# First expert's rows from one-hot products instead of a gather, in a two-layer decoder trunk with sorted experts

## What is computed

```python
for layer in range(2):
    u = rms_norm(h, norm_mix[layer]) * (1 + sc1) + sh1
    h = h + g1 * mixer(u)            # layer 0: windowed attention and convolution; layer 1: pooling
    u = rms_norm(h, norm_ffn[layer]) * (1 + sc2) + sh2
    h = h + g2 * grouped_moe(u)      # 16 experts, each token goes to 2 of one group of 4
return rms_norm(h, norm_final)

# grouped_moe, per expert e, for the tokens that chose it
hid = silu(t @ w_gate[e]) * (t @ w_up[e])      # 1024 -> 256
out = out + gates[:, e] * (hid @ w_down[e])    # 256 -> 1024
```

## Time and profile before

| | |
|---|---|
| median of 3 runs | 689.59 us (689.57 to 692.98) |
| profiled execution | 691.79 us, span 690.10 us |
| TensorE busy | 636.4 us (92%) |
| VectorE busy | 358.3 us (52%) |
| ScalarE busy | 171.5 us (25%) |
| GpSimd busy | 96.9 us (14%) |
| mean granted clock of TensorE | 0.965 of full |

### The profile page before, as it was taken

The page is one execution under the profiler, slowest core; times in us unless marked ns, Lnnn a source line. Parts: engine busy times, 40 slices in busy tenths (PEclk is TensorE's granted clock), DMA queues, the critical chain, the costliest instruction groups (busy, mean ns, idle before and its releaser), DMA issues. The chain is left out here.

```text
span 690.1 us, 8415 instructions
## 1 busy us (share of the span) xinstructions
PE 636.4 (92%) x2897; PEld 328.6 (48%) x2897; DVE 358.3 (52%) x714; ACT 171.5 (25%) x437; POOL 96.9 (14%) x84
## 2 busy tenths in 40 slices
PE   4899989999899995889999999999678999999994
PEld 3455434444444442445455554468345455555441
DVE  4117698799996237863432222264776233223325
ACT  5000322323333421211122211242421122122223
POOL 0010001000000004113132312100021212222210
PEclk9999989999999996989999999999989999999997
DMA  9999998878889415799999998374789899999726
GB/s 326 361 367 371 384 318 289 328 263 293 311 307 393 160 64 186 249 410 312 322 345 371 359 321 272 92 274 183 305 304 393 278 309 354 370 367 364 253 41 244
DMA packets 68568, 203.76 MB, mean 295 GB/s; under 512 B 9633, under 2 KB 18965, under 8 KB 68524
## 3 DMA queue, kind: packets, MB, share of 16 engines
q1 hardware_dynamic: 58836, 183.63, 72.3%
q0 software_dynamic: 9040, 18.87, 11.4%
q10 hardware_dynamic: 648, 0.71, 0.3%
HBM read 189.90 MB, written 23.11 MB: 309 GB/s over the span
## 5 line engine op out<-in xcount | busy, mean ns | idle before, releaser
L1877 PE MATMUL ps<-ring,work 128*128 128x512 f32 x288 | 127.8, 595 | 0.0
L949 DVE SCALAR_TENSOR_TENSOR acc<-adaw,cond,acc 128x1024 f32<-128x1024 f32 x70 | 89.8, 1283 | 8.5 <-DMA adaw<-in_w_ada_dram 6.6
L1701 PE MATMUL psY<-xu,ring 128*128 128x512 f32 x192 | 88.0, 612 | 0.0
L1877 PEld LDWEIGHTS ps<-ring,work 128*128 128x128 f32 x288 | 54.3, 191 | 67.1 <-issue 66.8
L1402 DVE TENSOR_TENSOR work<-work,ps 128x256 f32<-128x256 f32 (+1 forms) x32 | 11.9, 372 | 128.6 <-ACT work L854 92.7
L854 ACT ACTIVATE work<-ps 128x256 f32<-128x256 f32 (+1 forms) x32 | 11.0, 344 | 237.7 <-PE ps L1877 175.6
L1915 PE MATMUL psY<-ring,work 128*128 128x512 f32 x144 | 69.8, 630 | 0.0
L1701 PEld LDWEIGHTS psY<-xu,ring 128*128 128x128 f32 x192 | 36.4, 195 | 45.4 <-issue 45.2
L613 POOL DMA_INDIRECT h_dram<-work x20 | 33.2, 1662 | 152.7 <-DVE work L1432 75.4
L847 ACT ACTIVATE work<-psA,modc,scl 128x128 f32<-128x128 f32 (+1 forms) x120 | 42.5, 434 | 48.2 <-PE psA L1854 46.6
L1432 DVE SCALAR_TENSOR_TENSOR work<-psY,work,gbc 128x512 f32<-128x512 f32 x40 | 28.2, 747 | 44.1 <-PE psY L1915 44.1
(11 more groups left out here) (266 smaller groups left out, 782.1 us busy)
## 6 DMA issues: line engine op xcount, KB each, us to landing
adaw<-in_w_ada_dram SPq DMA_DIRECT2D x84, 512.0 KB, 5.3
ring<-in_w_gate_dram SPq DMA_DIRECT2D x48, 512.0 KB
ring<-in_w_up_dram SPq DMA_DIRECT2D x48, 512.0 KB
ring<-in_w_down_dram SPq DMA_DIRECT2D x48, 512.0 KB
xu<-in_w_gate_dram SPq DMA_DIRECT2D x16, 512.0 KB
xu<-in_w_up_dram SPq DMA_DIRECT2D x16, 512.0 KB
xu<-in_w_down_dram SPq DMA_DIRECT2D x16, 512.0 KB
work<-in_w_ada_dram SPq DMA_DIRECT2D x12, 512.0 KB, 9.9
```

The costliest lines, as they stand in the source:

```text
L949: dve.scalar_tensor_tensor(total, adaw[:, n % ABUF, :], cond[:, k:k + 1], total if k else brow[:, :], ALU.mult, ALU.add).then_inc(mac_step, 1)
L1701: ins = pe.matmul(bank, wt, uT[:, k, :], start=(k == 0), stop=(k == KD - 1))
L1877: ins = pe.matmul(gu_ps[j % 2][:, :].rearrange("p (a f) -> p a f", a=2), xgT[:, j % 2, k, :], w_gu(j % 4)[:, :, k, :], start=(k == 0), sto ...
```

## The change

Position 0's rows are no longer gathered and turned. VectorE writes a float32 one-hot of expert 0 (`first_hot`, 128x512, in `brow`), and TensorE multiplies each strided 128x128 piece of `xhat` with it: for each of 8 channel blocks 4 products, one for each tile, summed in PSUM. That gives the turned rows at once. These 32 products stand in `route`, with `token_table(0)` ahead of the fourth block; `first_banked` lets ScalarE start after four blocks. The order of the one-hots and of the tables is now position 1 first, then 0, so that position 1, still gathered, is first in line. `tokens(l, 1)` moves behind VectorE's first half. The last `keep_clock` matmuls go. The memset of `xg` is done in two parts, the first when the mix has read three tiles, the second when it has read the fourth, ahead of GpSimd's wait for `h`. SyncE stores `h` of a tile when `h` is ready and the normed rows of the tile before behind it, and waits for the products before it loads weights over `xhat`. In `first_product` of position 0 the wait for VectorE's half comes at k = 4. The load of the final norm's row counts on `gbc_in` now.

```diff
-HOT = [(0,), (1,), (2, 3), (4, 6), (5,), (7,), (8, 10), (9,), (11,), (12, 13), (14,), (15,)]
-TABLE = [(0,), (1,), (2, 3), (4, 5, 6, 7), (8, 9, 10, 11, 12, 13, 14, 15)]
+HOT = [(1,), (0,), (2, 3), (4, 6), (5,), (7,), (8, 10), (9,), (11,), (12, 13), (14,), (15,)]
+TABLE = [(1,), (0,), (2, 3), (4, 5, 6, 7), (8, 9, 10, 11, 12, 13, 14, 15)]
...
-HOT_BY_TABLE = [1, 2, 3, 6, 12]
+HOT_BY_TABLE = [2, 3, 4, 7, 13]
+HOTS = len(HOT) + 1
...
+        first_hot = brow[:, 0:T * P].rearrange("p (t s) -> p t s", t=T)
...
-                for t in range(T):
-                    sp.wait_ge(xhat_ready, (2 * l + 1) * T + t + 1)
-                    sp.dma_start(h_dram[l][t * P:(t + 1) * P, :], h[:, t, :]).then_inc(h_stored, 16)
-                    sp.dma_start(xhat_dram[l][t * P:(t + 1) * P, :], xhat[:, t, :]).then_inc(xhat_stored, 16)
+                for t in range(T + 1):
+                    if t < T:
+                        sp.wait_ge(h_ready, l * T + t + 1)
+                        sp.dma_start(h_dram[l][t * P:(t + 1) * P, :], h[:, t, :]).then_inc(h_stored, 16)
+                    if t:
+                        sp.wait_ge(xhat_ready, (2 * l + 1) * T + t)
+                        sp.dma_start(xhat_dram[l][(t - 1) * P:t * P, :], xhat[:, t - 1, :]).then_inc(xhat_stored, 16)
...
                 sp.wait_ge(ids_ready, l + 1)
+                sp.wait_ge(xT_banked, l * E + 1)
...
                     load_cols(1)
 
+                    parts = xg.rearrange("p b d -> p (b d)").rearrange("p (c s) -> p c s", s=SEQ)
+                    pool.wait_ge(mix_banked, 2 * (T - 1))
+                    pool.memset(parts[:, :, 0:(T - 1) * P], 0.0).then_inc(xg_clear, 1)
+                    pool.wait_ge(mix_banked, 2 * T)
+                    pool.memset(parts[:, :, (T - 1) * P:SEQ], 0.0).then_inc(xg_clear, 1)
                 pool.wait_ge(h_ready, T * (l + 1))
...
-                    pool.memset(xg[:, :, :], 0.0).then_inc(xg_clear, 1)
-                    pool.wait_ge(xg_clear, 1)
+                    pool.wait_ge(xg_clear, 2)
...
-                for e in range(E):
+                for e in range(1, E):
...
+                dve.tensor_tensor(first_hot, cst[:, C_SLOT:C_SLOT + P].unsqueeze(1).broadcast_to([P, T, P]),
+                                  posm[:, :, 0:1].broadcast_to([P, T, P]), ALU.is_equal).then_inc(onehot_ready, 1)
                 one_hots(l, 0)
                 tokens(l, 0)
                 one_hots(l, 1)
-                tokens(l, 1)
...
                 xT_half(0, 0, 0)
+                tokens(l, 1)
                 room(l)
...
-                token_table(l, 0)
-                keep_clock(1)
+                first_rows_in(l)
+
+            def first_rows_in(l):
+
+                pe.wait_ge(xhat_ready, (2 * l + 2) * T)
+                pe.wait_ge(onehot_ready, l * HOTS + 1)
+                for k in range(KD):
+                    if k == 3:
+                        token_table(l, 0)
+                    for t in range(T):
+                        src = xhat[:, t, :].rearrange("p (a k) -> p k a", k=KD)[:, k, :]
+                        ins = pe.matmul(turned_ps(0)[:, k * P:(k + 1) * P], src, first_hot[:, t, :],
+                                        start=(t == 0), stop=(t == T - 1))
+                    if k == KD // 2 - 1:
+                        ins.then_inc(first_banked, 1)
+                ins.then_inc(xT_banked, 1)
                 token_table(l, 1)
...
-                    pe.wait_ge(xT_dve, l * E + e + 1)
+                    if e:
+                        pe.wait_ge(xT_dve, l * E + e + 1)
...
+                            if e == 0 and k == KD // 2:
+                                pe.wait_ge(xT_dve, l * E + 1)
                             if e == 0 and k == 5:
                                 token_table(l, 2)
...
-                keep_clock(2)
-                turn_in(0, 0, 0)
                 turn_in(1, 1, 0)
                 first_product(0, 0, 0)
```

More of the change, by code:

```diff
@@ L309, in trunk @@
         back_banked, back_added = sem("back_banked"), sem("back_added")
-        nfin_in = sem("nfin_in")
+        first_banked = sem("first_banked")
         out_ready, out_stored = sem("out_ready"), sem("out_stored")
@@ L584, in _ @@
                     pool.dma_start(nfin, norm_final.rearrange("(a d) -> a d", a=1).partition_broadcast(P)
-                                   .rearrange("p a d -> p (a d)")).then_inc(nfin_in, 16)
+                                   .rearrange("p a d -> p (a d)")).then_inc(gbc_in, 16)
                 if l == 0:
@@ L842, in xT_half @@
                 def xT_half(e, j, i):
-                    act.wait_ge(xT_banked, l * E + e + 1)
+                    if e == 0:
+                        act.wait_ge(first_banked, l + 1)
+                    else:
+                        act.wait_ge(xT_banked, l * E + e + 1)
                     n = H64 if is_half(e, j) else P
@@ L1456, in expert_loop @@
                     one_hots(l, i)
-                dve.wait_ge(gbc_in, 16 * (2 * l + 2))
+                dve.wait_ge(gbc_in, 16 * (3 * l + 2))
                 for a in range(2):
@@ L1529, in _ @@
                 expert_loop(l)
-            dve.wait_ge(nfin_in, 16)
             for t in range(T - 1):
@@ L1811, in route @@
                 ins.then_inc(pos_ready, 1)
-                token_table(l, 0)
-                keep_clock(1)
+                first_rows_in(l)
[12 more added lines that the diff above has]
+                ins.then_inc(xT_banked, 1)
                 token_table(l, 1)
             def token_table(l, i):
-                pe.wait_ge(onehot_ready, l * len(HOT) + HOT_BY_TABLE[i])
+                pe.wait_ge(onehot_ready, l * HOTS + HOT_BY_TABLE[i])
                 if i >= 2:
@@ L1843, in turn_in @@
                 def turn_in(e, j, i):
-                    pe.wait_ge(xg_in[j % 4], 16 * (l * (E // 4) + i + 1))
+                    pe.wait_ge(xg_in[j % 4], 16 * (l * (E // 4 - (j % 4 == 0)) + i + (j % 4 != 0)))
                     if not isinstance(e, int) or l * E + e > 1:
```

## The result

The changed kernel is slower: 698.07 us, median of 20 runs (694.55 to 701.86), against 691.91 us for the kernel before, 20 runs (687.54 to 698.38). The ratio is 1.010, 95% interval 1.008 to 1.0121, so 5.5 to 8.4 us. 688.8 us was forecast, in a range of 685.0 to 692.5; the time lies outside, on the other side of no change. The kernel before came out 2.3 us above the median of three that the forecast started from, so the differences tell more: -0.8 us was forecast, +6.9 is measured by the ratio.

What follows compares the result with a forecast made beforehand. TensorE's own work bounds the expert loops, so gains must come from the stretch ahead of each. Layer 0 -0.3 us and layer 1 -0.5 sum to -0.8, from median 689.59 to 688.8 us; range 685.0 to 692.5.

Steps and rivals of the forecast that it cites:

- the price of a product: TensorE's strided float32 128x128x128 products: 0.22 us each, 2.64 us for 12 ahead of the table, 7.0 for all 32.
- so the products are ready in time: In routing: products and a table take about 7.7 us from the first one-hot's end, sorting 8.7, so VectorE stays last.
- F: The end of the first one-hot comparison on VectorE (`first_hot` after the change), from which the forecast counts its chains.
- rival 1: TensorE's clock holds, as layer 0's idle stretch shrinks: -4.5 us, 685.1 us; chance 0.17.
- rival 3: The stall is not the memset's and nothing is saved: +3.3 us, 692.9 us; chance 0.16.
- VectorE's chain: From first one-hot's end to the table at k = 5: 15.78 us at high clock, where 14.00 and 17.96 were.
- The memset: Layer 0 routing: splitting GpSimd's memset frees VectorE's CAST and the addition behind it of a 4.3 us stall; 4.1 taken.
- The bound of 0.9 for the second part: Second memset part, beside the last `mix_in`: costed at nothing, with 0.9 us as upper bound.
- The clock: TensorE's clock is low when the products begin: costs 2.0 us in layer 0 and 1.7 in layer 1.
- h first: SyncE storing h before the normed rows costs and gives nothing by itself.
- TensorE's wait: At `token_table(2)`, k = 5 of the first expert: about 2 us idle in both layers, where 0.32 was.
- Everything behind it unchanged: Everything behind `token_table(2)` keeps its distance to it, so that event's shift carries unchanged to the end.

Runs made afterwards that it cites:

- experiment 1: Changed kernel with each product loading 128 channels side by side instead of every eighth (position 0's output wrong): 688.76 us, ratio 0.9974 to the kernel before.
- experiment 4: Kernel of experiment 6 with positions 0 and 1 turned by plain products with the identity instead of transposes: 690.47 us, one run.
- experiment 5: Each part alone on the kernel before: memset in two parts 688.13 us (0.9947), h stored first 687.34 (0.993), products 702.09 (1.0152).
- experiment 6: Kernel before with memset in two parts and h stored first, without the products (position 0 gathered and turned): 683.12 us, ratio 0.9888.

## Why the prediction was wrong

**The step that failed** is the price of a product, 0.22 us with "The turns of L1854 load the same stride". It is 0.48 us. Of the two rows taken, L1635 was the right operation with the wrong stride, and L1854 the right stride with the wrong operation (experiments 1 and 4). Twelve products ahead of the table took 5.81 us instead of 2.64, all 32 about 15.5 instead of 7.0.

The prediction had the rule that would have said so, the Trainium skill (SBUF — State Buffer, Door 1, SBUF "cachelines"): at least two hits for each 16-byte line. It was set aside because of the transposes. The trace agrees with it: two elements a line are free, one a line takes 9.42 to 9.61 us where side by side takes 4.82. The page gives no figure; by these runs it is a factor of two at the full clock, on load and stream.

**Then the order of the chains turned.** The sentence "so the products are ready in time" put VectorE last, with the sorting 8.7 us and the products 7.7 us after F. With 0.48 us a product they end 285.85 - 270.17 = 15.7 us after F. VectorE waited 3.9 us for them after having waited 5.6 for the table (its own tail behind them, 286.05 to 293.03, took 7.0 us where the sum had 3.41 + 0.40 + 3.28 = 7.1), and the range, "from rival 1 to the nearer half of rival 3", had no case for TensorE being last. With the weights side by side the stretches come out at 17.15 and 18.26 us. The 12 products ahead of the table take 4.02 and 5.26 us there, 1.38 and 2.62 more than 2.64, and 15.78 plus that is 17.16 and 18.40. So VectorE's chain holds but for that one price.

**The memset**: right. 4.1 us were taken, the CAST and the addition lost their 4.3. The bound of 0.9 for the second part wasn't needed.

**The clock**: it was low where forecast, at 0.71 over the first products of layer 0 and 0.57 over those of layer 1, and cost nothing there: 24 instructions took 5.81 and 5.82 us, 0.242 each, and at the full clock it is 0.240. In the run of the products alone the same 24 had 0.50 throughout in layer 0 and took 5.86 us. It cost in experiment 1, where the first 24 took 4.02 us at 0.67 and 5.26 at 0.50. That is 4.0 us more than 2 x 2.64, near the 3.7 forecast, but shared out otherwise: 1.4 and 2.6 where 2.0 and 1.7 were taken.

**h first**: nothing in the changed kernel, as forecast; but on a kernel that gathers position 0 it is worth about as much as the memset, 4.8 and 3.7 us with intervals that overlap (experiment 5). The prediction looked at it with the products only. With the memset's edit beside it, it brings layer 1 to 14.90 us with the gather (experiment 6), below the 15.78 that the products were to reach.

**TensorE's wait** at the table: about 2 us forecast, 1.65 measured in both layers. That is luck: the forecast took the difference between VectorE's chain and the gather's, but both now start behind the last product. The wait that was meant shows in experiment 1, with 1.61 and 1.51 us.

**Everything behind it unchanged**: not quite. TensorE's +9.5 us became 6.9 in the runs. At the end of layer 1 the chain that ended last runs through the scatters of results; before, and after:

```profile
666.11 6.09 DMA h_dram<-work
```

```profile
675.65 6.01 DMA h_dram<-work
```

The scatter starts 9.5 us later, while the table of layer 1 is 523.82 - 513.01 = 10.8 us later in the same two profiles: 1.3 us are taken up there. The stretch between the tables took up another 1.2 (293.03 to 500.95 against 285.91 to 495.05). In the other runs these stretches differ by as much either way, so this split isn't settled.

**The rivals.** Rival 3 named the right side for the wrong reason: the stall did go. None had the products as the cause; it stood only among what would make the forecast wrong, without a chance.

## What to carry to other kernels

Price an operation by a row of the same operation with the same operand strides; if no row has both, take the slower reading of each as a bound and give the case a chance of its own. In plain instructions of 128 columns a float32 operand whose elements lie 16 or 32 bytes apart halved TensorE's rate at the full clock, so lay it out side by side, or leave it to a transpose. When a change bundles edits, measure them apart: here two small ones were worth 7.7 us, and the large one cost 10.5 alone. Ask too whether the small ones already take what the large one is for: with them, the products would have lost even without the price of the stride (experiments 1 and 6).

## What the runs showed of the hardware

- Plain float32 instructions of 128 columns come 0.12 us apart with a step of one or two elements (40 in 4.82 us at a granted clock of 0.94, in 4.79 at 1.00). With a step of eight elements they come 0.24 apart at 1.00 and at 0.50 alike (24 in 5.86 us, the products alone), with a step of four 0.24 at 1.00; streamed with a step of eight, 0.235. At a clock of 0.50 the side-by-side ones are 0.22 apart (24 in 5.26 us, experiment 1), so there the stride costs a tenth and not a factor of two.
- A transpose with a step of eight isn't slowed: 193 ns a load, as a plain one side by side (192), where a plain one takes 335 of the same buffer. Why is open.
- Without a memset beside it the CAST is not always at 0.25 us: in experiment 6 it takes 0.60 and in experiment 1 0.52. Both times it ends 0.1 us after one of GpSimd's DMA instructions ends and the next begins (262.07 us in experiment 6, the rows are below; 262.22 in experiment 1). Beside the memset it likewise ends 0.1 us after the memset's end (265.74 and 265.63). In the changed kernel and with the memset alone such a DMA instruction runs beside it too, and it takes 0.25. So GpSimd's DMAs seem able to hold VectorE by 0.3 us, of the prediction's bound of 1.0; no run was made to separate them.

```profile
261.56 0.60 DVE L1197 CAST work<-cst 128x128 bf16<-128x128 f32 x1
...
262.07 0.56 POOL L567 DMA_DIRECT2D acc<-mod_dram  x1
```
